# The first norm of a decoder trunk: modulation rows loaded, summed and used by groups of channels

## What is computed

```python
D_MODEL, SEQ, DEPTH = 1024, 256, 2

def rms_norm(x, g):
    y = x * lax.rsqrt(jnp.mean(x * x, axis=-1, keepdims=True) + NORM_EPS)
    return y * g

def modulate(x, g, shift, scale):
    return rms_norm(x, g) * (1 + scale[:, None, :]) + shift[:, None, :]

def short_conv_mixer(h, w_in, w_conv, w_out):
    b_gate, c_gate, v = jnp.split(h @ w_in, 3, axis=-1)
    ...
    return (b_gate * conv) @ w_out

c_act = jax.nn.silu(c)
for i in range(DEPTH):
    mod = c_act @ ada_w[i] + ada_b[i]                     # ada_w[i]: 1024 x 6144
    sh1, sc1, g1, sh2, sc2, g2 = jnp.split(mod, 6, axis=-1)
    h = modulate(x, tok_norm[i], sh1, sc1)
    y = short_conv_mixer(...) if i == 0 else mla_mixer(...)
    x = x + g1[:, None, :] * y
    h = modulate(x, ch_norm[i], sh2, sc2)
    x = x + g2[:, None, :] * peer_mixer(...)
```

## Time and profile before

| | |
|---|---|
| median of three runs | 1941.47 us (1936.61 to 1942.4) |
| the profiled execution | 1939.04 us, of which its span is 1937.3 us |
| around the span | 1.74 us |
| TensorE products busy | 98% of the span |
| VectorE / ScalarE / GpSimd busy | 82% / 52% / 15% |
| HBM traffic | 369.53 MB read, mean 191 GB/s |

### The profile page before, as it was taken

One profiled execution on the slowest core, in us unless ns is written; L12 is line 12 of the kernel. 1 busy time (PEld: TensorE's weight loads), 2 busy tenths in 40 slices (PEclk: granted clock), 3 DMA queues, 4 the chain that ended last, 5 costly groups with the idle time before them and its releaser, 6 DMA issues.

```text
span 1937.3 us, 39849 instructions
## 1 busy us (share of the span) xinstructions
PE 1901.5 (98%) x13067; PEld 1662.8 (86%) x13067; DVE 1597.6 (82%) x3091; ACT 1015.0 (52%) x1638; POOL 294.5 (15%) x172
## 2 busy tenths in 40 slices
PE   8999999999999999999999999999999999999998
PEld 7999898888888888887899998988888888888877
DVE  6748999999999999997765489988888888888866
ACT  4354455555555555554455544455555555555553
POOL 3877300000000000000052572000000000000000
PEclk8999999999999999999998999999999999999999
DMA  9965445776777777777732454456566655566554
GB/s 365 354 202 171 160 143 165 221 224 226 218 225 222 232 220 226 220 225 228 231 107 74 131 163 135 139 154 183 176 182 178 180 177 181 178 180 181 176 185 140
DMA packets 104151, 371.76 MB, mean 192 GB/s; under 512 B 11392, under 2 KB 13824, under 8 KB 103680
## 3 DMA queue, kind: packets, MB, share of 16 engines
q1 hardware_dynamic: 96000, 341.26, 55.9%
q0 software_dynamic: 8064, 29.36, 5.0%
HBM read 369.53 MB, written 1.05 MB: 191 GB/s over the span
## 4 chain that ended last, share of the span: by engine, by line
PE 84%; DVE 9%; DVEq 2%; DMA 1%; POOL 1%; issue 1%; ACT 1%; SPq 0%; POOLq 0%; ACTq 0%
PE bank L590 36%; PE bank L576 18%; PE bank L578 9%; PE bank L439 4%; PE bank L441 4%; PE bank L440 4%; PE bank L604 2%; DVE w_lo L1242 2%; DVE hot_b L1468 1%; POOL w_lo L1198 1%; DVEq L1474 1%; DVE arena L1359 1%; PE bank L831 1%; DVE arena L1326 1%; PE bank L459 1%
## 5 line engine op out<-in xcount | busy, mean ns | idle before, releaser
L890 ACT CAST w_hi<-raw 128x1024 fp32r<-128x1024 f32 (+1 forms) x603 | 630.8, 1046 | 290.8 <-PE bank L590 108.5
L1242 DVE TENSOR_TENSOR w_lo<-raw,w_hi 128x1024 fp32r<-128x1024 f32 x493 | 603.3, 1224 | 135.3 <-PE bank L578 59.3
L576 PE MATMUL bank<-act_two,w_hi 128*128 128x512 f32 x1536 | 548.2, 397 | 0.0
L578 PE MATMUL bank<-act_two,w_lo 128*128 128x256 f32 x1536 | 430.6, 280 | 0.0
L576 PEld LDWEIGHTS bank<-act_two,w_hi 128*128 128x128 f32 x1536 | 288.5, 188 | 69.0
L590 PE MATMUL bank<-w_hi,wt_hi 128*128 128x512 f32 x1024 | 328.3, 401 | 3.3 <-DVE wt_lo L1507 2.6
L439 PE MATMUL bank<-act_two,w_hi 128*128 128x256 f32 x1060 | 307.4, 290 | 14.7 <-DVE w_lo L1242 12.0
L590 PE MATMUL bank<-w_lo,wt_hi 128*128 128x512 f32 x1024 | 318.9, 393 | 0.0
L590 PE MATMUL bank<-w_hi,wt_lo 128*128 128x512 f32 x1024 | 316.1, 390 | 0.0
L440 PE MATMUL bank<-act_two,w_hi 128*128 128x256 f32 x1060 | 299.9, 283 | 0.0
L441 PE MATMUL bank<-act_two,w_lo 128*128 128x256 f32 x1060 | 299.9, 283 | 0.0
(11 more groups left out here) (232 smaller groups left out, 1962.9 us busy)
## 6 DMA issues: line engine op xcount, KB each, us to landing
raw<-in_u_panels SPq DMA_DIRECT2D x256, 512.0 KB, 3.7
raw<-in_v_panels SPq DMA_DIRECT2D x256, 512.0 KB, 3.6
raw<-in_panels SPq DMA_DIRECT2D x81, 512.0 KB, 4.2
ada<-in_ada_rows POOLq DMA_DIRECT2D x56, 512.0 KB, 4.7
arena<-in_ada_rows SPq DMA_DIRECT2D x40, 512.0 KB, 7.1
raw<-in_panels SPq DMA_DIRECT2D x6, 384.0 KB, 3.1
arena<-in_subkeys SPq DMA_DIRECT2D x2, 1024.0 KB, 5.9
xT<-in_xT SPq DMA_DIRECT2D x1, 1024.0 KB, 6.8
```

Source lines behind the costliest of these rows:

```text
L576: pe.matmul(bank[:, 0:2 * T], w_hi[:, slots[0], w], act_two[:, :, a], start=(k == 0), stop=False, skip_group_check=True)
L578: mm = pe.matmul(bank[:, 0:T], w_lo[:, slots[1], w], act_hi[:, a], start=False, stop=(k == KB - 1), skip_group_check=True)
L890: nc.scalar.copy(w_hi[:, slot, 0:width], raw[:, slot, 0:width]).then_inc(hi_done, 1)
L1242: dve.tensor_tensor(w_lo[:, lo_slot, 0:width], raw[:, slot, 0:width], w_hi[:, slot, 0:width].bitcast(F32), ALU.subtract).then_inc(lo_done, 1)
```

## The change

The sixteen rows are loaded and summed in four groups (`FIRST_ROWS`): scales 0, 1 and shifts 0, 1; scales 2, 3 and shifts 2, 3; scales 4 to 7 and shifts 4, 5; shifts 6, 7. VectorE makes gains and shifts after each group. The reciprocal of the rms stands after the seventh row. GpSimd multiplies x by 1/rms in four pieces of two blocks. ScalarE does gain and shift of a block one behind the other; its casts of panels 0 and 1 stand between blocks 3 and 4. TensorE takes the first pair in steps of two blocks, with 36 products of zeros ahead instead of 50, and 8 more before the last step.

```diff
--- before.py
+++ after.py
@@ -99,6 +99,8 @@
 PAIRS_IN_ORDER = ("conv_in", "conv_out", "sel0", "mla_in", "mla_out", "sel1")
 QB_ORDER = (4, 5, 0, 1, 2, 3)
 TWO_PI = 2.0 * np.pi
+FIRST_ROWS = (((0, 2), (0, 2)), ((2, 4), (2, 4)), ((4, 8), (4, 6)), ((8, 8), (6, 8)))
+FIRST_ORDER = [r for scales, shifts in FIRST_ROWS for r in [KB + k for k in range(*scales)] + list(range(*shifts))]
 PI_1 = 6.28125
 PI_2 = float(np.float32(np.floor((TWO_PI - PI_1) * 2.0 ** 21) / 2.0 ** 21))
 PI_3 = float(np.float32(TWO_PI - PI_1 - PI_2))
@@ -385,16 +387,18 @@
                         sp.dma_start(posi, pos_in.partition_broadcast(P)).then_inc(s_pos, 16)
 
             sp.dma_start(crow[:], c_in.partition_broadcast(P)).then_inc(s_c, 16)
-            load_ada(0, KB, 0)
+            def first_rows(n0, n1):
+                for n in range(n0, n1):
+                    load_ada(n, FIRST_ORDER[n], n % ADA)
+
+            first_rows(0, 4)
             sp.dma_start(xT[:], xT_in).then_inc(s_const, 16)
             sp.dma_start(con[:, 0:C_MASK], con_in[:, 0:C_MASK]).then_inc(s_const, 16)
             sp.dma_start(vec[:], vec_in).then_inc(s_const, 16)
-            for j in range(1, KB):
-                load_ada(j, KB + j, j % ADA)
+            first_rows(4, 10)
             for j in range(2):
                 load_panel("conv_in", j)
-            for j in range(KB):
-                load_ada(KB + j, j, (KB + j) % ADA)
+            first_rows(10, 2 * KB)
             for j in range(2, RAW):
                 load_panel("conv_in", j)
             with sp.Fori(0, 2) as it:
@@ -471,11 +475,13 @@
                         mm = pe.matmul(PAN[p][:, 0:T], w_hi[:, s[0], w], acts[1][k], start=False, stop=(k == KB - 1))
                     mm.then_inc(pan_done, 1)
 
-            def first_pair(hi, lo, count, wait, acts=norm_act):
+            def first_pair(hi, lo, count, wait, acts=norm_act, step=KB // 2, fill=0):
 
                 slots = []
-                for half in range(2):
-                    pair_hi(hi, count, slots, acts, half * KB // 2, (half + 1) * KB // 2, wait if half == 0 else None)
+                for k0 in range(0, KB, step):
+                    if k0 == KB - step:
+                        busy(STAT, fill)
+                    pair_hi(hi, count, slots, acts, k0, k0 + step, wait if k0 == 0 else None)
                 pair_lo(lo, count, slots, acts)
 
             def conv_pair():
@@ -868,8 +874,8 @@
             pe.wait_ge(s_const, 48)
             token_square_sums(1)
             spread_rstd(1)
-            busy(PAN[0], 50)
-            first_pair(norm_hi, norm_ready, 0, lambda p: wait_panel("conv_in", p))
+            busy(PAN[0], 36)
+            first_pair(norm_hi, norm_ready, 0, lambda p: wait_panel("conv_in", p), step=2, fill=8)
             for j in range(2, 24):
                 full_panel("conv_in", j)
             conv_pair()
@@ -1053,15 +1059,17 @@
             rms_of(1)
             act.wait_ge(rstd_spread, 1)
             nc.scalar.copy(rstd[:, T:2 * T], STAT[:, T:2 * T]).then_inc(rstd0_copied, 1)
-            for j in range(2):
-                split_hi("conv_in", j)
-            act.wait_ge(gains0, 1)
             for k in range(KB):
-                act.wait_ge(by_rstd, 1 + k * 2 // KB)
+                if k == KB // 2:
+                    for j in range(2):
+                        split_hi("conv_in", j)
+                act.wait_ge(by_rstd, 1 + k // 2)
+                act.wait_ge(gains0, 1 + min(k // 2, 2))
                 c = slice(k * T, (k + 1) * T)
                 nc.scalar.activation(act32[:, c], act32[:, c], ACT.Copy, scale=gain[:, k:k + 1]).then_inc(by_gain, 1)
-            act.wait_ge(by_gain, KB)
-            normalise(1, 0, 0)
+                act.wait_ge(by_gain, k + 1)
+                act.wait_ge(scaled, k + 1)
+                nc.scalar.activation(act_hi[:, c], act32[:, c], ACT.Identity, bias=mod[:, k:k + 1]).then_inc(norm_hi, 1)
             split_hi("conv_in", 2)
             for it in range(2):
                 for b in range(4):
@@ -1206,11 +1214,11 @@
 
             pool.wait_ge(s_const, 48)
             pool.wait_ge(rstd0_copied, 1)
-            for half in range(2):
-                c = slice(half * KB * T // 2, (half + 1) * KB * T // 2)
+            for g in range(KB // 2):
+                c = slice(2 * g * T, 2 * (g + 1) * T)
                 by_block = lambda a: a.rearrange("p (k t) -> p k t", t=T)
                 pool.tensor_tensor(by_block(act32[:, c]), by_block(xT[:, c]),
-                                   rstd[:, T:2 * T].unsqueeze(1).broadcast_to([P, KB // 2, T]), ALU.mult).then_inc(by_rstd, 1)
+                                   rstd[:, T:2 * T].unsqueeze(1).broadcast_to([P, 2, T]), ALU.mult).then_inc(by_rstd, 1)
             for j in range(24):
                 split_lo("conv_in", j)
             for j in range(KB):
@@ -1768,24 +1776,29 @@
             dve.sem_inc(sc_used, 2)
             dve.sem_inc(evac["conv_in"], 2)
             dve.wait_ge(s_silu, 1)
-            for j in range(KB):
-                ada_row(j, 0, 0, j)
-                if j == 3:
-                    inverse_rms(1)
-            dve.wait_ge(s_const, 48)
-            scales = conv_sum[:, 0:KB]
-            dve.drain()
-            dve.tensor_tensor(scales, scales, vec[:, V_ADAB + KB:V_ADAB + 2 * KB], ALU.add)
-            dve.drain()
-            dve.scalar_tensor_tensor(out=gain[:], in0=scales, scalar=1.0, in1=vec[:, V_TOK:V_TOK + KB],
-                                     op0=ALU.add, op1=ALU.mult).then_inc(gains0, 1)
-            dve.drain()
+            row = 0
+            for scales, shifts in FIRST_ROWS:
+                n = scales[1] - scales[0]
+                m = shifts[1] - shifts[0]
+                for j in range(n + m):
+                    ada_row(row, 0, 0, j)
+                    row += 1
+                    if row == 7:
+                        inverse_rms(1)
+                dve.wait_ge(s_const, 48)
+                dve.drain()
+                if n:
+                    some = conv_sum[:, 0:n]
+                    dve.tensor_tensor(some, some, vec[:, V_ADAB + KB + scales[0]:V_ADAB + KB + scales[1]], ALU.add)
+                dve.tensor_tensor(mod[:, shifts[0]:shifts[1]], conv_sum[:, n:n + m],
+                                  vec[:, V_ADAB + shifts[0]:V_ADAB + shifts[1]], ALU.add).then_inc(scaled, m)
+                dve.drain()
+                if n:
+                    dve.scalar_tensor_tensor(out=gain[:, scales[0]:scales[1]], in0=some, scalar=1.0,
+                                             in1=vec[:, V_TOK + scales[0]:V_TOK + scales[1]], op0=ALU.add, op1=ALU.mult
+                                             ).then_inc(gains0, 1)
+                    dve.drain()
             dve.wait_ge(s_silu, 2)
-            for half in range(2):
-                for j in range(4):
-                    ada_row(KB + 4 * half + j, 0, 0, j)
-                modulation(4 * half, 4, conv_sum)
-                dve.sem_inc(scaled, 4)
             normalised_lo(1, 0, 0)
 
             def conv_low(k):
```

## The result

| | before | after |
|---|---|---|
| median (20 runs of each) | 1938.78 us (1936.61 to 1945.14) | 1943.34 us (1940.72 to 1949.35) |
| the profiled execution | 1939.04 us, span 1937.3 | 1943.13 us, span 1940.7 |

The ratio after to before is 1.0021, 95% interval [1.0012, 1.0029]. That is some 4 us slower: less than the 0.3% that the prediction had set as what can be told, but with 20 runs of each it can be told from no change. The forecast was 1943.5 and "same".

A forecast was written before the change was run, and what follows sets the result against it. TensorE, nearly always busy behind the first pair, hands the start's delay on; late `w_lo`, half clock and fillers put panel 2 at 43.8 against 40.44, +3.3 us kept: 1942.3 from the profiled execution, named 1943.5, range 1937.5 to 1948.5.

The forecast's parts named there:

- Steps 1 to 4: Start, up to GpSimd's x by 1/rms: squares 13.4, sums 6.8 us, reciprocal 21.9, last shifts 34.8, GpSimd done 28.7.
- Steps 5 and 6: ScalarE's blocks at 0.94 us each delay the casts to 28.9 to 30.9, GpSimd's second `w_lo` to 34.8, 7.0 later.
- the reserve of 4.7 us: First pair before the change: how much later `w_lo`, ready at 27.85, could have come without delaying the pair.
- Step 7: TensorE's first pair: idle 33.2 to 34.9 for `w_lo`, half clock 36.6 to 40.0, late fillers 2.8 us, `pair_lo` ends 43.6.
- The sum: Start to panel 2: steps added up to 43.8 against 40.44, +3.4 us, of which +3.3 reaches the end.
- rival A: First pair: the 1.7 us stop does not bring the clock down; panel 2 +1.9, time 1940 to 1941; chance 0.24.
- the 43.8 that was named as a sign: Start of panel 2 if the forecast is right, against 40.44 before.
- Step 8: Panel 2's `w_lo` waits for panel 0's last `pair_hi` product at 41.2, ends 43.7 level with `pair_lo`; panel 2 at 43.8.
- the start's loss is handed on nearly whole: Behind the first pair TensorE lacks 0.3 us in 71 us, so at most that is given back.
- the +2.5 to +4.2: Whole kernel: band of the change's cost that counts as the forecast itself, chance 0.51.

The follow-up runs named there:

- Experiment 6: The kernel before with rows 1 to 3 loaded ahead of xT, the rest of the change left out; single run 1941.13 us.
- Experiment 7: The changed kernel with 46 products of zeros at the start instead of 28, bridging TensorE's idle time before the sums; single run 1949.51 us.
- Experiment 3: The changed kernel with ScalarE's casts of panels 0 and 1 ahead of all blocks; 1940.70 us.
- experiment 1: The changed kernel run again with no edit; 1946.93 us.
- experiment 2: The changed kernel without the eight products of zeros before the last step of the first pair; 1943.11 us.
- experiment 4: The changed kernel with xT, constants and vectors loaded ahead of rows 1 to 3 again; 1944.05 us, ratio to before 1.0019.
- experiment 5: The changed kernel with xT ahead of rows 1 to 3, and GpSimd waiting for all eight remainders before panel 2's `w_lo`; 1939.53 us.
- experiment 8: Changed kernel: xT first, no late fillers, earlier reciprocal, remainders of blocks 0 to 3 and panel 2's cast; 1941.66 us, ratio 1.0016.
- experiment 9: Experiment 8's kernel with five products of zeros ahead of block 4 and four ahead of block 6; 1939.24 us, ratio to before 1.0006.
- experiment 10: The kernel before with 14 more small activations on ScalarE; the two PEER stages took 717.12 and 850.51 us.
- experiment 11: The kernel before with 11 more one-column clears on VectorE; the two PEER stages took 717.59 and 850.99 us.

## Why the prediction was right

**Steps 1 to 4 held.** Squares at 13.55 (13.4), sums 6.8 us long at 0.50 (6.8), reciprocal at 22.04 (21.9), GpSimd from 24.04 in 5.05 us (23.9; I took 4.8 and not the 5.1 that I had from the nearest width). The last shifts came at 35.00 (34.8). Experiment 6 shows the load order as the cause of the late reciprocal. Experiment 7 shows that the long idle time ahead of the sums cost them 3.2 us. Two slips in the working changed nothing: behind the reciprocal stand row 7 and eight more rows, not nine, and one more round of small operations than in before, not three. What makes the shifts late is the nine sums that wait for a reciprocal 5.7 us later.

**Steps 5 and 6 held, and they are the mechanism.** A block took 0.94 as worked out, casts at 29.15 and 30.10 (28.9, 29.9), second `w_lo` at 35.01 (34.8): the reserve of 4.7 us was overdrawn, and TensorE waited 1.50 us for it (1.7). Experiment 3 moved the casts forward, and panel 2 came 1.02 us earlier.

**Step 7 was a coin.** The sum took the fall of the clock as given, and left the other case to rival A at 0.24. The fall held in experiments 1 and 2, not in the profiled after; there rival A's +1.9 came out as +2.2. So in that execution panel 2 came at 42.64, not at the 43.8 that was named as a sign, though TensorE did wait for `w_lo` and not for `act_hi`. The late fillers are on the path, as said: 1.8 us of it (39.39 less 37.55), where the forecast had 2.8 with five of them at half clock. The sum also took 40.44 as what before does; it has a fall in it, and the two padded executions of that kernel without one came to 40.80 and 40.93 by the clash of VectorE and GpSimd, which the prediction did not see.

**Step 8 held in kind.** `w_lo` of panel 2 starts on the last product of panel 0's `pair_hi` and ends 0.2 behind `pair_lo`.

**What the sum lacked, and where luck came in.** The spans of the two profiled executions differ by 3.4 us: 2.2 at panel 2, 0.8 more up to the keys, 0.5 in the first PEER stage, -0.5 in the attention, 0.4 in the second. Outside the span there are 0.7 more. Not in my sum were the waits behind the pair (they vary: from panel 2 to the keys 72.93 us passed in before, 73.74 in after, 72.82 in experiment 1), the losses from VectorE's instruction count, and the time around the span. By luck they are about as large as the fall of the clock that didn't come. I had said that the start's loss is handed on nearly whole, and it is; but the change acts elsewhere as well. With the forecast's own clock the start alone would be +3.7.

The forecast's 1943.5 lies 0.2 from the median, and that too is partly luck. It was +3.3 on a level put midway between 1939.04 and 1941.47; 20 runs of before put the level at 1938.78. Measured as a difference the change costs 4.1 us by the ratio and 4.6 by the medians, at the upper edge of the +2.5 to +4.2 that the prediction called its forecast. From the traces one gets 3.0 to 3.6 at the keys, 1.0 in the two PEER stages and 0.7 around the span, 4.7 to 5.3, with the attention, which varies by more than that, left out. What the time around the span is made of stays open: it is 2.0 to 2.9 us in the runs of after and of experiments 1 to 5, 8 and 9, but 1.71 in experiment 7, which is made from after as well.

**The noise.** In the attention the clock falls in some executions more often than in others: the same work, at 907 to 1081 us in before, took 171.7 us in experiment 6, 173.8 in before, 178.5 in experiment 7. So single times (1949.51 in 7, 1941.13 in 6) can say the reverse of their starts. The mean granted clock over 910 to 1080 of experiment 7, and of before:

```profile
910.00:1080.00 170.00, 168.06 (x1001) 148.83 (x1000) 109.14 (x218) 88.20 (x152) 44.06 (x25) 0.94 0.46 141
```

```profile
910.00:1080.00 170.00, 167.80 (x1050) 149.87 (x1049) 109.05 (x224) 92.90 (x161) 48.09 (x27) 0.96 0.43 133
```

## What to carry to other kernels

Before loads are regrouped so that a consumer can start sooner, count the reserve of every other chain that the new order delays; here moving 1.6 MB ahead of xT delayed 1/rms by 5.7 us, and a `w_lo` that nobody had been waiting for became the last to come. Price a fall of the clock as a chance, from several executions of one kernel, and ask of the baseline too whether it has one in it. Put products of zeros only where TensorE's data is not there yet: eight of them ahead of data that was there cost 1.8 us. When VectorE's two-input work and GpSimd's work fall due together, put them in order on purpose.

## What the hardware did that I had not expected

- **VectorE and GpSimd shut each other out.** A remainder of 128x256 took 2.58 to 2.60 us instead of 0.48 in experiments 4, 6, 7, 10 and 11, each time begun 0.1 to 0.4 us behind a GpSimd `w_lo`. Near a tie the recorded starts don't tell which of the two loses: at the same distance of 0.13 us VectorE lost in 10 and 11 and won in before.
- **Sums of one column** ran whole at clock 1.00 behind products of zeros (32 in 3.6 us, experiment 7), and whole at 0.50 when the clock had fallen before them (6.8 us, after). In before they began at 1.00 and ended at 0.50.
- **A few small instructions act far away.** Eleven clears of 0.06 us each at the start made VectorE pause 0.49 us longer some 890 us later, and the two PEER stages 0.4 to 0.5 us longer each (experiment 11 against before).
- **The clock's fall differs between executions.** It came in one execution of the changed kernel behind a stop of 1.60 us and not in another behind 1.50. It came in before behind 2.54 us and not in experiment 11 behind 2.51.
